# Latent preparation of an RWKV-7 mixer: norms ahead of partial products, one product to ScalarE, bonus and lower exclusive sums to GpSimd

## The chip, the core and the metric

The kernel runs on one core of a Trainium2 chip. The core's engines work side by side, each on its own queue of instructions, and wait for one another on semaphores: TensorE (PE; its weight loads are shown apart as PEld), VectorE (DVE), ScalarE (ACT), GpSimd (POOL), and SyncE (SP), which here only issues transfers. The time is the device time of one execution in microseconds (us); the median of several runs counts.

## The reference, cut to what matters

The program computes a block with a retention mixer, an RWKV-7 mixer and a mixture of experts, and behind it two layers of another model. The change touches one stage: it prepares, for the 256 latent tokens and 8 heads of 64, the operands of the RWKV-7 scan. In the reference this is:

```python
def rwkv_prepare(u, w0, w2, a0, a2, g2, k_k, k_a, r_k):
    ...
    def decay(wl, w0_d, w2_d):
        w_log = -jax.nn.softplus(-(w0_d + jnp.tanh(wl) @ w2_d)) - 0.5
        return heads(jnp.exp(-jnp.exp(w_log)))

    iclr = jax.nn.sigmoid(a0 + al @ a2)
    kk = heads(k * k_k)
    kk = kk / jnp.maximum(jnp.linalg.norm(kk, axis=-1, keepdims=True), 1e-12)
    k_mod = heads(k * (1.0 + (iclr - 1.0) * k_a))
    r, v = heads(r), heads(v)
    bonus = (jnp.sum(r * k_mod * r_k.reshape(RWKV_HEADS, RWKV_DIM), axis=-1, keepdims=True) * v).reshape(B, T, -1)
    ...
    return (r, decay(wl_f, w0[0], w2[0]), decay(wl_b, w0[1], w2[1]), k_mod, v, -kk, kk * heads(iclr), g_f, g_b, bonus)
```

The scan is done in chunks of 64 tokens, so the decays' logarithms are summed within each chunk, inclusive and exclusive, forwards for one direction and backwards for the other. Beside this, the stage makes `silu(c) @ w_mod` for the second half of the modulation.

## The kernel before

The program is a row of stages. Each opens a block in which every engine has its own list of instructions, written out by hand in the order in which it runs, and all engines meet at a barrier between stages. The stage at issue is `rwkv_prepare_stage` (from L1001), called at L1597 for the latent tokens; behind it comes `rwkv_chunks_stage` (L1294), the scan itself.

All tiles are float32 with channels on the 128 partitions. The 8 heads are worked off in 4 pairs p. Partitions 0 to 63 (`lo`) hold the forward direction of a decay, 64 to 127 (`hi`) the backward one. The steps, by engine:

- TensorE: the decays' pre-activations (L1075), those of `iclr` (L1079), the sums of squares of the keys (L1086, products with 2 columns). Then `partial(0)` and `partial(1)`, each 8 products of a weight slot (512 columns, 32 output rows, helper L183) for the modulation; the spread of the 16 norms over the partitions (L1099); `partial(2)` and `partial(3)`; `double(0)` (L1122 to L1135), which copies a pair of operands into PSUM for both directions; 16 products with one column that turn the partials (L1144); `double(1)` to `double(3)`; at the end one product to keep the engine busy (helper L162). `double(1)` waits until ScalarE has copied the result of L1144 (`second_read`).
- ScalarE: sigmoids of the decays (L1160), the squares of the keys (L1168), the sigmoids of `iclr` (L1173), after a load of another function table the square root (L1176), copies of the partials (L1180), after another table load for each pair three exponentials (L1198, L1199, L1201), which wait for `sums_ready`.
- VectorE: keys times k_k (L1250); `scan(p)`, the inclusive sums (L1215) and two small copies of the chunks' totals (L1221, L1222); `sums(p)`, the exclusive sums: one subtraction for `lo` (L1228), two for `hi` (L1230) and an addition for `hi` (L1233); the norm's clip and reciprocal (L1255, L1256, then `norm_ready`); the normed keys (L1259), `bb` (L1263), `kmod` in two steps (L1265, L1266); the bonus products (L1269), blocks 0 and 1 there, 2 and 3 behind `sums(2)`; `scale(p)` (L1243, L1244, L1246), four products of a doubled pair in PSUM with the exponentials. `scale(p)` waits for the doubling and for the exponentials of its pair; `scan(p+2)` and `sums(p+2)` come behind `scale(p)`, because there are two buffers of sums only.
- GpSimd: the product of silu (L1057), and three small operations on the modulation (L1060 to L1064).
- SyncE: three small transfers and the loads of weight slots as they come free (L121).

## Time and profile before

| | us |
|---|---|
| median of 3 runs | 1829.65 |
| lowest, highest | 1828.99, 1830.1 |
| the profiled execution | 1836.64 |
| its span | 1834.6 |
| TensorE busy | 1645.0 |
| VectorE busy | 727.8 |
| ScalarE busy | 371.8 |
| GpSimd busy | 77.2 |

The profiled execution's mean granted TensorE clock was 0.959 of full speed; a granted clock of 1.00 is 2.4 GHz, of 0.50 is 1.2 GHz. The stage runs from 374.08 us of the span, the first instruction of TensorE and of VectorE in it, to 413.74, the end of VectorE's last product. A timeline merges neighbouring instructions of the same line, xN is their number; TensorE does each float32 product as two instructions in the record. The idle time in brackets is the engine's own just before the row, with what ended it.

### The profile page before, as it was taken

To read this page: it belongs to the slowest core of one execution; us is meant where nothing else is said; L and a number is where in the kernel's file an instruction comes from. 1 tells how busy PE (TensorE), PEld (TensorE's weight loads), DVE (VectorE), ACT (ScalarE), POOL (GpSimd) and SP (SyncE) were. 2 spreads that over 40 slices of the span, in tenths; PEclk is the share of its full clock that TensorE was granted. 3 is DMA by queue.
4 is the path that set the end of the run, shared out by engine and by line. 5 is a ranking of instruction groups with operands and counts; after the bars stand their busy time and mean duration, and the time that the engine had idled before them with its cause. 6 is when DMAs were issued, how large, how long until landed. Compare 5 with 4: busy or idle time off the path is not lost.

```text
span 1834.6 us, 29021 instructions
## 1 busy us (share of the span) xinstructions
PE 1645.0 (90%) x12736; PEld 1064.6 (58%) x12736; DVE 727.8 (40%) x1326; ACT 371.8 (20%) x870; POOL 77.2 (4%) x94
## 2 busy tenths in 40 slices
PE   9999998988999876676666999999999999999998
PEld 5665557948835322121112386769984577679963
DVE  2005465675563100000000235556664255646663
ACT  2110133544422201010000224320010225210000
POOL 0000003304220000000000000000000000000000
PEclk9999998998998999888888999999999999999999
DMA  8621020040086999999999932224454532135450
GB/s 368 252 100 47 11 110 2 4 184 3 4 346 265 429 430 431 430 430 431 430 430 431 397 149 92 92 92 179 150 224 180 205 132 72 68 120 202 184 195 23
DMA packets 35583, 381.90 MB, mean 208 GB/s; under 512 B 6977, under 2 KB 10433, under 8 KB 12673
## 3 DMA queue, kind: packets, MB, share of 16 engines
q1 hardware_dynamic: 35458, 380.04, 51.2%
q8 instruction: 101, 1.65, 0.4%
q14 instruction: 24, 0.20, 0.0%
HBM read 378.98 MB, written 1.05 MB: 207 GB/s over the span
## 4 chain that ended last, share of the span: by engine, by line
PE 45%; DMA 17%; DVE 3%; ACT 2%; issue 1%; DVEq 0%; PEldq 0%
DMA arena<-in_w_moe 17%; PE psum L2959 15%; PE psum L3021 7%; PE psum L2340 6%; PE psum L2343 3%; PE psum L2009 2%; PE psum L162 2%; PE psum L2493 2%; PE psum L2481 1%; PE psum L2041 1%; PE psum L1976 1%; PE psum L2460 1%; PE psum L1956 1%; PE psum L2369 0%; PE psum L2446 0%
## 5 line engine op out<-in xcount | busy, mean ns | idle before, releaser
L2959 PE MATMUL psum<-arena 128*128 128x128 f32 x1408 | 165.2, 275 | 1.7 <-DVE arena L3157 1.7
L2959 PEld LDWEIGHTS psum<-arena 128*128 128x128 f32 x1408 | 161.0, 192 | 2.0 <-issue 2.0
L2157 DVE COPY arena<-psum 128x512 f32<-128x512 f32 x16 | 11.1, 691 | 373.2 <-PE psum L2009 373.2
L2959 PE MATMUL psum<-arena,weight_ring 128*128 128x128 f32 x1056 | 127.9, 277 | 6.3 <-DVE arena L3195 4.2
L2959 PEld LDWEIGHTS psum<-arena,weight_ring 128*128 128x128 f32 x1056 | 123.4, 194 | 8.6 <-issue 5.8
L1371 PE MATMUL psum<-arena 64*64 64x64 f32 x3328 | 109.0, 222 | 10.9 <-POOL arena L1542 8.1
L2340 PE MATMUL psum<-arena,weight_ring 128*128 128x256 f32 x512 | 118.5, 382 | 0.3 <-ACT arena L2555 0.3
L1371 PEld LDWEIGHTS psum<-arena 64*64 64x64 f32 x3328 | 101.5, 137 | 17.3 <-POOL arena L1542 8.6
L2340 PEld LDWEIGHTS psum<-arena,weight_ring 128*128 128x128 f32 x512 | 94.5, 189 | 19.1 <-issue 2.9
L2009 PE MATMUL psum<-arena 128*32 128x512 f32 x480 | 68.4, 701 | 36.8 <-DMA arena<-in_w_moe 36.8
L3140 DVE TENSOR_TENSOR arena<-weight_ring 128x1024 f32<-128x1024 f32 (+1 forms) x72 | 81.2, 1128 | 51.0 <-PE psum L3021 51.0
L2009 PE MATMUL psum<-weight_ring,arena 128*32 128x512 f32 x544 | 68.3, 632 | 27.7 <-DMA weight_ring<-in_w_moe 27.2
L3021 PE MATMUL psum<-arena 128*128 128x512 f32 x176 | 78.7, 593 | 0.4 <-DVE arena L3140 0.4
L1976 PE MATMUL psum<-arena 128*128 128x512 f32 x128 | 61.0, 620 | 18.8 <-ACT arena L2092 16.9
L2343 PE MATMUL psum<-weight_ring,arena 128*128 128x512 f32 (+1 forms) x192 | 72.3, 524 | 2.7 <-DVE arena L2796 2.7
L2080 ACT ACTIVATE arena<-psum 128x256 f32<-128x256 f32 x16 | 6.1, 384 | 288.7 <-PE psum L2021 288.7
L2009 PEld LDWEIGHTS psum<-arena 128*32 128x32 f32 x480 | 14.2, 118 | 85.1 <-DMA arena<-in_w_moe 56.0
L2009 PEld LDWEIGHTS psum<-weight_ring,arena 128*32 128x32 f32 x544 | 16.0, 113 | 77.4 <-DMA weight_ring<-in_w_moe 41.1
L467 PE MATMUL psum<-arena,weight_ring 128*128 128x256 f32 x256 | 59.0, 393 | 1.3 <-PEq L208 1.3
L3021 PE MATMUL psum<-weight_ring,arena 128*128 128x512 f32 x132 | 60.1, 592 | 0.0
L162 PE MATMUL psum<-arena 128*128 128x512 f32 x106 | 54.2, 649 | 5.4 <-DVE arena L1246 4.4
L3021 PEld LDWEIGHTS psum<-arena 128*128 128x128 f32 x176 | 33.3, 190 | 43.2 <-issue 41.1
(498 smaller groups left out, 2333.7 us busy)
## 6 DMA issues: line engine op xcount, KB each, us to landing
weight_ring<-in_w_moe SPq DMA_DIRECT2D x50, 2048.0 KB, 44.9
arena<-in_w_moe SPq DMA_DIRECT2D x46, 2048.0 KB, 44.3
weight_ring<-in_w_in SPq DMA_DIRECT2D x23, 2048.0 KB, 11.4
weight_ring<-in_w_mod SPq DMA_DIRECT2D x12, 2048.0 KB, 11.8
weight_ring<-in_w_gate SPq DMA_DIRECT2D x12, 2048.0 KB, 7.9
weight_ring<-in_w_up SPq DMA_DIRECT2D x12, 2048.0 KB, 7.9
weight_ring<-in_w_down SPq DMA_DIRECT2D x12, 2048.0 KB, 7.9
weight_ring<-in_w_out SPq DMA_DIRECT2D x6, 2048.0 KB, 7.8
```

The lines of the kernel that those rows point to most:

```text
L162: nc.tensor.matmul(K.ps[:, bank, :], K.ident, K.ident.unsqueeze(1).broadcast_to([P, 4, P]), start=True, stop=True, skip_group_check=True)
L467: last = nc.tensor.matmul(bank[:, 0:T], w[:, k, P * b:P * b + P], hT[:, k, T:2 * T], start=(k == 0), stop=(k == KT - 1), skip_group_check= ...
L1371: last = nc.tensor.matmul(K.ps[half[d], bank, to:to + HD], lhs(d, h), rhs(d, h), start=True, stop=True, skip_group_check=True)
L1956: last = nc.tensor.matmul(spot(q, d), K.h2[:, t, P * d:P * d + P], sel[:, t, cols], start=(t == 0), stop=(t == 1), skip_group_check=True)
L1976: last = nc.tensor.matmul(K.ps[:, 2 * t + n, :], scatter_to[:, e // 4 % 2, e % 4, P * t:P * t + P], parts[:, n, :], start=(e == 0), stop=( ...
L2009: last = nc.tensor.matmul(K.ps[strip(j), 4, :], xsT[:, e // 4 % 2, k, strip(e % 4)], w[:, i, j, :], start=(k == 0), stop=(k == KT - 1), sk ...
L2340: last = nc.tensor.matmul(K.ps[:, bank, 0:T], w[:, k, P * b:P * b + P], hT[:, k, :], start=(k == 0), stop=(k == KT - 1))
L2343: last = nc.tensor.matmul(K.ps[:, bank, 0:width], hT[:, k, P * b:P * b + P], w[:, k, 0:width], start=(k == 0), stop=(k == KT - 1))
L2493: last = nc.tensor.matmul(K.ps[:, out_bank(t, n), :], K.mixT[:, k, P * t:P * t + P], ws[n][:, k, :], start=(g == 0 and k == 0), stop=(g == ...
L2959: last = nc.tensor.matmul(K.ps[:, bank, P * n:P * n + P], lhs, rhs, start=(n == 0 and k == 0 and name in ("m1", "m5", "m6")), stop=(k == 3 ...
L3021: return nc.tensor.matmul(K.ps[:, int(name[1]) - 1, :], lhs, rhs, start=(j == 0), stop=(j == NFT // 2 - 1), skip_group_check=True)
L3140: nc.vector.tensor_tensor(out, x, y, op).then_inc(sums_ready, 1)
```

## The change

- TensorE: in place of `partial(0)` and `partial(1)` one product to keep it busy (helper L162) stands ahead of the spread of the norms; all four partials stand behind the spread.
- ScalarE: four Identity activations write a new tile `rate` = iclr * k_a + (1 - k_a), between `iclr` and the square root; behind the square root four Copy activations write r * r_k into `K.prod`; the copy of `partial(0)` moves behind the exponentials of pair 0.
- VectorE: `kmod` is one product, rate * k. The bonus products are gone. `sums(p)` has no subtraction for `lo`, and waits before its last addition for GpSimd (`below_ready`).
- GpSimd: 1 - k_a (128x4) first; after silu, `below(p)`, the subtraction for `lo` (64x512), once `scan(p)` is done; ahead of `below(2)` and of `below(3)` one half each of the bonus, `K.prod` times `kmod` (128x512).

```diff
@@ GpSimd
+                def below(p):
+                    pool.wait_ge(scanned, p + 1)
+                    if p >= 2:
+                        pool.wait_ge(scaled, p - 1)
+                    nc.gpsimd.tensor_tensor(exc[lo, p % 2], inc[lo, p % 2], pair(sg, p)[lo], ALU.subtract).then_inc(below_ready, 1)
+
+                nc.gpsimd.tensor_tensor(rest, K.ones[:, 0:4], K.vecs[:, 2, :], ALU.subtract).then_inc(rest_ready, 1)
                 pool.wait_ge(sig_ready, 1)
                 nc.gpsimd.tensor_tensor(K.silu, K.silu, sig, ALU.mult).then_inc(silu_ready, 1)
+                for p in range(2):
+                    below(p)
+                pool.wait_ge(r_scaled, 4)
+                pool.wait_ge(ready["k"], 1)
+                for p in range(2, 4):
+                    nc.gpsimd.tensor_tensor(K.prod[:, 2 * p - 4:2 * p - 2, :], K.prod[:, 2 * p - 4:2 * p - 2, :],
+                                            kmod[:, 2 * p - 4:2 * p - 2, :], ALU.mult)
+                    below(p)
@@ TensorE
-                if lat:
-                    pe.wait_ge(silu_ready, 1)
-                    for c in range(2):
-                        pe.wait_ge(sg_ready, 2 * c + 2)
-                        partial(c)
+                keep_busy(nc, K, 3, 1)
                 pe.wait_ge(norm_ready, 1)
...
                 if lat:
+                    pe.wait_ge(silu_ready, 1)
                     pe.wait_ge(sg_ready, H)
-                    for c in range(2, 4):
+                    for c in range(4):
                         partial(c)
@@ ScalarE
+                act.wait_ge(rest_ready, 1)
+                act.wait_ge(iclr_ready, 4)
+                for b in range(4):
+                    nc.scalar.activation(rate[:, b, :], iclr[:, b, :], ACT.Identity, bias=rest[:, b:b + 1],
+                                         scale=K.vecs[:, 2, b:b + 1]).then_inc(rate_ready, 1)
                 act.wait_ge(ss_made, 1)
...
-                if lat:
-                    keep_part(0)
+                for b in range(4):
+                    nc.scalar.activation(K.prod[:, b, :], K.rT[:, b, :], ACT.Copy, scale=K.vecs[:, 3, b:b + 1]).then_inc(r_scaled, 1)
                 for p in range(4):
                     if lat and p == 1:
+                        keep_part(0)
                         keep_part(1)
@@ VectorE
-                    link(nc.vector.tensor_tensor(e[lo], i[lo], g[lo], ALU.subtract))
...
+                    dve.wait_ge(below_ready, p + 1)
                     nc.vector.tensor_tensor(i[hi], e[hi], g[hi], ALU.add).then_inc(sums_ready, 1)
...
-                dve.wait_ge(ready["b"], 1)
-                link(nc.vector.scalar_tensor_tensor(iclr, iclr, -1.0, spread(2), ALU.add, ALU.mult))
-                nc.vector.scalar_tensor_tensor(kmod, iclr, 1.0, k, ALU.add, ALU.mult).then_inc(ready["k"], 1)
...
-                bonus(0)
-                bonus(1)
+                dve.wait_ge(rate_ready, 4)
+                nc.vector.tensor_tensor(kmod, rate, k, ALU.mult).then_inc(ready["k"], 1)
                 for p in range(4):
                     scale(p)
                     if p < 2:
                         scan(p + 2)
                         sums(p + 2)
-                    if p == 0:
-                        bonus(2)
-                        bonus(3)
```

TensorE's instructions from the sums of squares to the first doubling, before (`arena` is on-chip memory, `weight_ring` the weight slots):

```order
L1086 MATMUL psum<-arena 128x2 x8
L183 MATMUL psum<-weight_ring,arena 32x512 x16
L1099 MATMUL psum<-arena 64x128 x16
L183 MATMUL psum<-weight_ring,arena 32x512 x16
L1122 MATMUL psum<-arena 128x256 x2
```

And the same place after; L1106, L1115 and L1139 are the former L1086, L1099 and L1122:

```order
L1106 MATMUL psum<-arena 128x2 x8
L162 MATMUL psum<-arena 128x512
L1115 MATMUL psum<-arena 64x128 x16
L183 MATMUL psum<-weight_ring,arena 32x512 x32
L1139 MATMUL psum<-arena 128x256 x2
```

Sixteen of the partials' products moved from ahead of the norms' spread to behind it, and one product of 512 columns stands in their place.

GpSimd's instructions in the stage after (L1067 is 1 - k_a, L1069 silu, L1065 `below`, L1075 the bonus); before there were only those that are now L1069 and L1080 to L1084:

```order
L1067 TENSOR_TENSOR arena<-arena 128x4
L1069 TENSOR_TENSOR arena<-arena 128x8 [waits stage1_dve_step]
L1065 TENSOR_TENSOR arena<-arena 64x512 [waits stage5_s1_scanned] x2
L1075 TENSOR_TENSOR arena<-arena 128x512 [waits stage1_squares_summed,stage5_s1_r_scaled]
L1065 TENSOR_TENSOR arena<-arena 64x512 [waits stage1_hT_made,stage5_s1_scanned]
L1075 TENSOR_TENSOR arena<-arena 128x512
L1065 TENSOR_TENSOR arena<-arena 64x512 [waits stage1_hT_made,stage5_s1_scanned]
L1080 TENSOR_TENSOR arena<-arena 128x16 [waits stage5_s1_second_read,stage1_latent_scaled_by_act]
```

The second L1075 has no wait of its own: it follows `below(2)` at once. (Semaphores are named after the first stage that used them.)

## Rows read from the trace of the kernel before

**Rows 1.** Chain of waits, 480 to 600 us: start, length (us), what; its first piece.

```profile
581.01 0.04 issue
```

**Rows 2.** The page: what the DMA engines moved, in 40 slices of 45.9 us.

```profile
GB/s 368 252 100 47 11 110 2 4 184 3 4 346 265 429 430 431 430 430 431 430 430 431 397 149 92 92 92 179 150 224 180 205 132 72 68 120 202 184 195 23
```

**Rows 3.** Timeline of TensorE: start, us, engine line op out<-in xcount [idle before <-releaser].

```profile
379.60 2.12 PE L1086 MATMUL psum<-arena 128*128 128x2 f32 x16
...
381.65 5.10 PE L183 MATMUL psum<-weight_ring,arena 128*32 128x512 f32 x32
...
386.68 1.97 PE L1099 MATMUL psum<-arena 128*64 128x128 f32 x32
...
388.58 3.64 PE L183 MATMUL psum<-weight_ring,arena 128*32 128x512 f32 x32
...
392.15 0.70 PE L1122 MATMUL psum<-arena 64*128 64x256 f32 x4
...
394.34 3.73 PE L1144 MATMUL psum<-arena 128*128 128x1 f32 x32
...
398.40 1.22 PE L1122 MATMUL psum<-arena 64*128 64x256 f32 x4 [0.32 <-issue]
...
411.40 1.56 PE L162 MATMUL psum<-arena 128*128 128x512 f32 x2 [4.44 <-DVE arena L1246]
```

**Rows 4.** Timeline of ScalarE, 379 to 384 us.

```profile
379.91 1.62 ACT L1173 ACTIVATE arena<-psum,arena 128x256 f32<-128x256 f32 x4
...
381.55 1.28 ACT L1176 ACT_TABLE_LOAD   x1
...
382.84 0.18 ACT L1176 ACTIVATE arena<-psum 128x16 f32<-128x16 f32 x1
```

**Rows 5.** Timeline of VectorE, 383 to 414 us.

```profile
383.14 0.17 DVE L1255 TENSOR_SCALAR arena<-arena 128x16 f32<-128x16 f32 x1 [0.62 <-ACT arena L1176]
...
394.55 0.69 DVE L1243 TENSOR_TENSOR arena<-psum,arena 128x512 f32<-128x512 f32 x1
...
397.14 1.23 DVE L1215 TENSOR_TENSOR_SCAN arena<-arena 128x512 f32<-128x512 f32 x1
...
399.52 0.88 DVE L1230 TENSOR_TENSOR arena<-arena 64x256 f32<-64x256 f32 x2
...
401.16 0.88 DVE L1269 SCALAR_TENSOR_TENSOR arena<-arena 128x256 f32<-128x256 f32 x2
...
402.27 0.69 DVE L1243 TENSOR_TENSOR arena<-psum,arena 128x512 f32<-128x512 f32 x1 [0.23 <-PE psum L1135]
...
408.87 0.69 DVE L1243 TENSOR_TENSOR arena<-psum,arena 128x512 f32<-128x512 f32 x1
...
412.47 1.27 DVE L1246 TENSOR_TENSOR arena<-psum,arena 128x512 f32<-128x512 f32 x2
```

**Rows 6.** Stretches: us, busy PE, PEld, DVE, ACT, POOL, then granted clock, DMA share, GB/s.

```profile
381.30:384.70 3.40, 3.40 (x19) 1.11 (x22) 2.61 (x8) 1.70 (x3) 0.00 (x0) 0.51 0.99 424
...
384.70:388.10 3.40, 3.40 (x46) 1.78 (x40) 1.04 (x2) 2.96 (x4) 0.00 (x0) 1.00 1.02 347
...
398.30:401.70 3.40, 3.30 (x20) 2.06 (x24) 3.16 (x9) 0.54 (x2) 0.95 (x3) 0.50 0.04 14
...
411.90:415.30 3.40, 1.70 (x8) 0.67 (x8) 1.84 (x4) 0.00 (x0) 0.00 (x0) 0.51 0.00 0
```

**Rows 7.** GpSimd's groups by line and shape: count, busy us, mean ns, idle before.

```profile
L1542 POOL TENSOR_TENSOR arena<-arena 128x512 f32<-128x512 f32 x40 | 43.6, 1091 | 33.4 <-PE psum L1371 33.1 <-ACT arena L1493 0.4
...
L1057 POOL TENSOR_TENSOR arena<-arena 128x8 f32<-128x8 f32 x1 | 1.1, 1082 | 22.5 <-ACT arena L1166 22.5
...
L1060 POOL TENSOR_TENSOR arena<-arena 128x16 f32<-128x16 f32 x1 | 0.2, 216 | 20.4 <-ACT arena L1191 20.4
```

**Rows 8.** Timelines of VectorE and of GpSimd, 525 to 537 us.

```profile
525.59 0.88 DVE L1872 SCALAR_TENSOR_TENSOR arena<-arena 128x256 f32<-128x256 f32 x2
...
531.92 2.35 POOL L1798 TENSOR_TENSOR arena<-arena 128x1024 f32<-128x1024 f32 x1 [16.88 <-ACT arena L1832]
...
532.36 4.71 DVE L1872 SCALAR_TENSOR_TENSOR arena<-arena 128x256 f32<-128x256 f32 x2
```

More of the change, by code:

```diff
@@ L1022, in rwkv_prepare_stage @@
     norm = A.temp(2, H)
+    rate, rest = A.temp(4, T), A.temp(4)
     tok = slice(T * s, T * s + T)
```

14 lines of the change are left out of this document (7 added, 7 removed).

## The prediction

> **What bounds the kernel now.** I read the waits first, then the timelines of the four engines between 374 and 414 us (the latent preparation), then the granted clock of the same stretch, and last the chain of waits. The chain as recorded starts only at 581.01 us [rows 1], so it says nothing about this stage; what the stage is worth has to be read from its own timelines. All engines leave it together through a barrier, no weight transfer is under way from 400 to 500 us (3 and 4 GB/s in the two slices behind it [rows 2]), and so I take every microsecond by which the last VectorE product (end 412.47 + 1.27 = 413.74 us [rows 5]) moves as one that the whole kernel moves.
>
> Within the stage two paths alternate. Up to 394.5 us they are balanced: TensorE does two partial products (381.65), the spread of the norms (386.68), two more partials (388.58) and the first doubling (392.15, over at 394.34) [rows 3]; VectorE ends its keys and bonus work at the same moment and starts scale(0) at 394.55 [rows 5]. Note what the first pair of partials does there: it fills the time in which TensorE would wait for the norms. From 394.55 on VectorE is the bound: it is busy to 413.74 but for one wait of 0.23 us on the second doubling [rows 5].
>
> **The change, part by part.** All of it is summed as the new start of scale(0), then the way from there to the end.
>
> *Root later on ScalarE.* Four Identity activations of 128x256 (the rate) go between the last iclr and the square root's table load. The four sigmoids of that size take 1.62 us, the load 1.28, the root 0.18 [rows 4]. Root done: 383.02 + 1.6 = 384.65; norm_ready after the clip and reciprocal: 383.60 + 1.6 = 385.2 [rows 4, 5]. Before, this hid under partials that ran until 386.7; now they are gone and it is bare.
>
> *Spread of the norms earlier.* It can start at 385.25 instead of 386.68. At the full clock it takes 1.97 us less a little overlap [rows 3], ending 387.2. The clock decides what is left of this. It falls at 381.3, after the 2-column products of L1086 [rows 3, 6]. Before, TensorE then worked without a gap and the clock was back at 384.7 [rows 6]. Now it has one warming product (1.56 us where the clock fell during it, more at half [rows 3]) and then nothing until 385.25. In the stretch of 411.9 to 415.3 it was likewise busy for only 1.70 of 3.40 us, and there the clock stayed at 0.50 until 418.7 [rows 6]. I take that: low until 388.1. Then 2.85 us give 1.42 us of work, the other 0.55 run at full clock, end 388.65, which is just where it ended before. So the 1.4 us that the reordering gives are taken back.
>
> *Four partials behind the norms instead of two.* Two take 3.64 us at full clock (388.58 to 392.15 plus the tail [rows 3]); four take 7.2 to 7.3. First doubling starts at 395.95 and ends 2.2 us later, at 398.15 (392.15 to 394.34 before [rows 3]). scale(0) starts at 398.2 instead of 394.55: **+3.65**. With the clock back at 384.7 it would be 387.2 + 7.3 + 2.2 = 396.7: **+2.2**. Weights for the partials are no new wait: the first four-slot read had none at 381.65, and all are read later than before.
>
> *Keys' rate by ScalarE, bonus by GpSimd.* VectorE loses one 128x1024 operation and the four bonus products (one pair 0.88 [rows 5]), about 3 us in all. The first two bonuses and the 128x1024 lie ahead of scale(0), where VectorE now waits for TensorE from about 392.5 to 398.2: worth nothing. The second pair lies after sums(2) and is 1.1 us with the wait behind it (401.16 to 402.27 [rows 5]): that is on the path.
>
> *Lower exclusive sums by GpSimd.* VectorE loses a 64x512 subtraction (0.7) per pair and gets a wait for GpSimd in its place; the next scale and ScalarE's exponentials queue behind that wait. GpSimd has done no such subtraction here. Nearest row: 128x512, 1.09 us [rows 7]. If both engines ran freely, GpSimd (0.05 + 1.09) would be done before VectorE's two copies and two upper subtractions (0.40 + 0.88), and a pair gains 0.7. But GpSimd's 128x8 product at 377.01 took 1.08 us where its 128x16 addition takes 0.22 [rows 7], as long as a scan of VectorE's runs (1.22, rows of the same form in [rows 5]), and VectorE's L1872, 0.88 for two, took 4.71 for two beside GpSimd's 128x1024 products [rows 8]. Operations of VectorE with two SBUF inputs and those of GpSimd take turns. Then a pair costs 0.05 + 1.09 + 0.88 + 0.7 = 2.8, against 2.76 before (398.37 to 401.13): nothing gained. In the trace no engine works on one half of the partitions while the other works on the other half, so both ends stay: 0 to -0.7 for each of pairs 2 and 3; I take 0, since the rows on turns are of these very kinds. (Pairs 0 and 1 end before anything waits for them.) The Trainium skill, page "SBUF — State Buffer", section "SBUF: two separate sides", says that the pair of ports which VectorE and GpSimd share is an exclusive lock held for the whole instruction, and that a VectorE operation with two SBUF inputs needs it. By that rule the partition halves don't matter and the end at 0 holds; without it the total below would be 0.7 less. The trace's 4.71 us agree.
>
> *The second bonus product in the way.* GpSimd issues prod(2:4), a 128x512 product, straight behind below(2). VectorE's two upper subtractions and the addition want the same turns: one of them gets 1.09 us later. So sums(2) costs 2.8 + 1.09 = 3.9 instead of 2.76 plus the bonus' 1.14: from scale(0) to scale(1) VectorE needs 3.82 (394.55 to the scan's end 398.37) + 3.9 = 7.75, before 7.72. Bounds -1.1 (no turn lost) to +0.
>
> *TensorE on the same stretch.* Between first and second doubling stand the 1-column products (394.34 to 398.07) and ScalarE's copy (to 398.4), 4.05 us, then the doubling, 3.65 us at the half clock (398.40 to 402.05) or 2.2 at the full one [rows 3]. The clock fell at 398.3 behind those thin products [rows 6] and will again. 7.7 us: it gates scale(1) at the same moment as VectorE. So even if GpSimd took no turn, scale(1) would start no earlier: **+0.05** at best estimate.
>
> *scale(1) to the end.* 6.60 us to scale(2) and 4.87 us to the end before [rows 5]; the same with turns taken, 5.9 and 4.87 without. **0** (or -0.7). ScalarE's four Copy activations for the bonus (1.6 us) lie at 384.7 to 386.3, and its exponentials for pair 0 are done by 389.5: hidden by 8 us. GpSimd's additions to the second modulation come after below(3) instead of at 398.4; they are used behind the next stage. Transfers on SP: the third and fourth w_mod loads are released up to 5 us later, into the 100 idle us.
>
> **Sum:** 3.65 + 0.05 + 0 = +3.7 us. The profiled execution has a span of 1834.6 us and a time of 1836.64; it would be 1840.3. On the median of the runs, 1829.65, it gives 1833.3. About 0.2% (3.66 us) is what a measurement of this kernel can tell from no change, so the forecast stands on that bound.
>
> **Rivals.**
> 1. *The clock is back at 384.7.* For: the stretch begins with full-array work. Against: row 411.90 [rows 6]. scale(0) +2.2; then VectorE bounds: +2.25, time 1831.9. Where GpSimd also takes no turns, +0.1 to +1.5: about 1830.4. Chance 0.22.
> 2. *Low until 388.1, but no turns.* +3.65 - 0.7 = +2.95: 1832.6. Chance 0.12.
> 3. *Slower: the clock stays low through the partials too.* Place: TensorE, 388.1 to 391.5. TensorE's work from 385.25 on would not bring it back. Price: 3.4 us at half, 1.7 lost, total +5.4: 1835.0. It decides if the granted clock is 0.5 after 388.1. For: the stretch starts with a gap, as none did here before the clock rose at 384.7. Against: the stretch of 381.3 was followed by the full clock with such 32-column products alone [rows 3, 6]. The Trainium skill, page "TensorE: Matmul & The Clock Gate", section "What's actually happening", has the throttled state as the default, released by activity. It gives no other time than this rival or the forecast. Chance 0.13.
> 4. *Faster, or the change doesn't bite on the path.* It needs GpSimd without turns, the clock back at 384.7 and thin products that don't lower it: 387.2 + 7.3 + 2.2, then 6.25, 5.9 and 4.87 us, end at 413.8, so +0.1; and beyond that the next stage, which now starts in the low stretch of 411.9 to 418.7, starting at the full clock, worth up to 3 us. Chance of faster by over 0.2%: 0.05.
>
> **How the numbers follow.** Forecast (low to 388.1, turns taken) 0.48, half of it on either side of +3.66. Same: 0.24 + 0.22 + 0.12 = 0.58; slower: 0.24 + 0.13 = 0.37; faster 0.05. The range goes from +0.2 (rival 1 at its cheap end) to +5.5 (rival 3): 1829.8 to 1835.2.
>
> **What would show it.** In the profile after: root at 384.65 and a gap of TensorE from 383.5 to 385.2; granted clock 0.5 from 381.3 to 388.1; scale(0) at 398.2 with VectorE idle 5 to 6 us ahead of it, released by TensorE; the upper subtractions after scan(2) stretched to 3 us in all; last scale ending near 417.4. The prediction is wrong if scale(0) starts before 396.5, if the upper subtractions take 0.88 us beside GpSimd's, or if the shift of 3.7 us at the stage's end isn't found at the kernel's end.

## The result, and the profile after

The changed kernel is slower: its time is 1.0034 of the time before, 95% interval 1.0022 to 1.0046, 12 runs of each on the same chip. That is +6.2 us (4.0 to 8.4). The medians were 1838.24 and 1832.12 us. Single runs of one kernel spread far more than the three that were shown ahead of the prediction: 1828.6 to 1838.2 before, 1832.0 to 1841.5 after. Its page begins:

```profile
span 1837.8 us, 29037 instructions
...
PE 1649.6 (90%) x12738; PEld 1071.2 (58%) x12738; DVE 726.0 (40%) x1317; ACT 375.4 (20%) x878; POOL 84.4 (5%) x101
```

The span is only 3.2 us longer than in the profiled execution before, but that one happened to be slow for its kernel (1836.64 us against a median of 1832.12). The stage itself tells more. It lasts from 374.18 to 420.73, 46.55 us; before it lasted 39.66. So +6.9 us arose in it. On the way to the kernel's end 3.7 us of that were given back in this pair, 2.9 of them between 520 and 534 us: the execution before waited 2.14 us there for a weight slot and then had its clock down for 3.4 us, the one after waited 0.88 us and had its clock up. Such differences come and go between executions: in the three other profiles of the changed kernel the same wait was 2.74, 2.35 and 2.07 us. The 12 runs average over them, and their +6.2 us come close to the stage's mean loss of 6.0 us (four profiles after, two before; below).

TensorE in the stage after, the answer to [rows 3] (start, us, engine line op, idle before and its releaser). L1106, L1115, L183, L1139 and L1161 are the 2-column products, the norms' spread, the partials, the doublings and the 1-column products:

```profile
379.71 2.09 PE L1106 MATMUL psum<-arena 128*128 128x2 f32 x16
...
381.66 2.06 PE L162 MATMUL psum<-arena 128*128 128x512 f32 x2
...
385.92 3.68 PE L1115 MATMUL psum<-arena 128*64 128x128 f32 x32 [2.20 <-DVE arena L1280]
...
389.53 8.08 PE L183 MATMUL psum<-weight_ring,arena 128*32 128x512 f32 x64
...
397.54 0.70 PE L1139 MATMUL psum<-arena 64*128 64x256 f32 x4
...
399.62 4.99 PE L1161 MATMUL psum<-arena 128*128 128x1 f32 x32
...
404.94 1.23 PE L1139 MATMUL psum<-arena 64*128 64x256 f32 x4 [0.32 <-issue]
```

The partials that used to fill 381.65 to 386.7 are one warming product of 2.06 us; then TensorE waits 2.20 us. The spread takes 3.68 us, not 1.97. The four partials end at 397.5, and the doubling that they hold up ends at 399.8. The 1-column products take 4.99 us where they took 3.73.

ScalarE, the answer to [rows 4]: the rate's four activations (L1195) take 2.08 us, and push the square root from 382.84 to 385.10.

```profile
380.00 1.61 ACT L1190 ACTIVATE arena<-psum,arena 128x256 f32<-128x256 f32 x4
...
381.71 2.08 ACT L1195 ACTIVATE arena<-arena 128x256 f32<-128x256 f32 x4
...
383.81 1.28 ACT L1198 ACT_TABLE_LOAD   x1
...
385.10 0.18 ACT L1198 ACTIVATE arena<-psum 128x16 f32<-128x16 f32 x1
```

VectorE, the answer to [rows 5]. L1267 is the first product of a scale, L1238 a scan, L1246 its second small copy, L1253 and L1257 the upper half of the sums, L1270 the last products of a scale:

```profile
385.40 0.17 DVE L1279 TENSOR_SCALAR arena<-arena 128x16 f32<-128x16 f32 x1 [1.56 <-ACT arena L1198]
...
399.83 0.69 DVE L1267 TENSOR_TENSOR arena<-psum,arena 128x512 f32<-128x512 f32 x1 [6.57 <-PE psum L1152]
...
402.42 1.22 DVE L1238 TENSOR_TENSOR_SCAN arena<-arena 128x512 f32<-128x512 f32 x1
...
403.88 1.14 DVE L1246 COPY arena<-arena 64x8 f32<-64x8 f32 x1
...
405.05 1.72 DVE L1253 TENSOR_TENSOR arena<-arena 64x256 f32<-64x256 f32 x2
...
406.80 0.69 DVE L1257 TENSOR_TENSOR arena<-arena 64x512 f32<-64x512 f32 x1
...
409.01 0.69 DVE L1267 TENSOR_TENSOR arena<-psum,arena 128x512 f32<-128x512 f32 x1 [1.52 <-PE psum L1152]
...
415.87 0.69 DVE L1267 TENSOR_TENSOR arena<-psum,arena 128x512 f32<-128x512 f32 x1
...
419.46 1.27 DVE L1270 TENSOR_TENSOR arena<-psum,arena 128x512 f32<-128x512 f32 x2
```

scale(0) starts at 399.83, after a recorded idle time of 6.57 us that TensorE's doubling ends; before it started at 394.55 without one. scale(1) waits 1.52 us for the second doubling, where it waited 0.23. The small copy L1246 took 0.17 us before and takes 1.14 now, the upper subtractions of pair 2 1.72 instead of 0.88.

GpSimd, the answer to [rows 7]. L1065 is the lower subtraction, L1075 half of the bonus:

```profile
382.55 1.26 POOL L1065 TENSOR_TENSOR arena<-arena 64x512 f32<-64x512 f32 x1 [3.01 <-DVE arena L1238]
...
403.72 1.25 POOL L1065 TENSOR_TENSOR arena<-arena 64x512 f32<-64x512 f32 x1 [9.22 <-DVE arena L1238]
...
404.94 1.08 POOL L1075 TENSOR_TENSOR arena<-arena 128x512 f32<-128x512 f32 x1
```

And the stretches around the clock's fall, the answer to [rows 6] (us, busy TensorE, its weight loads, VectorE, ScalarE, GpSimd, granted clock, DMA share, GB/s). The clock is at 0.50 for three stretches on end, 381.4 to 391.6, and once more from 401.9 to 408.7:

```profile
381.40:384.80 3.40, 2.31 (x5) 0.73 (x4) 2.37 (x3) 3.29 (x6) 1.26 (x1) 0.50 0.99 424
...
384.80:388.20 3.40, 2.29 (x22) 2.29 (x24) 1.97 (x5) 3.36 (x8) 0.00 (x0) 0.50 0.64 275
...
388.20:391.60 3.40, 3.40 (x26) 1.59 (x26) 1.92 (x2) 1.76 (x3) 0.00 (x0) 0.50 0.02 5
...
391.60:395.00 3.40, 3.40 (x36) 0.96 (x32) 1.66 (x2) 1.32 (x3) 1.09 (x1) 1.00 0.00 0
...
401.90:405.20 3.30, 2.98 (x16) 2.92 (x17) 3.09 (x5) 0.18 (x1) 1.48 (x2) 0.50 1.00 427
```

### The profile page after: what moved, and what is told of

It reads as the page before. It is cut to its first block, busy times and chain, and to the rows that moved or that the text cites. A ratio compares the mean times of both kernels' runs of the same rounds, so it can differ in the third digit from the quotient of the medians.

```text
span 1837.8 us, 29037 instructions
## 1 busy us (share of the span) xinstructions
PE 1649.6 (90%) x12738; PEld 1071.2 (58%) x12738; DVE 726.0 (40%) x1317; ACT 375.4 (20%) x878; POOL 84.4 (5%) x101
## 4 chain that ended last, share of the span: by engine, by line
PE 47%; DMA 15%; DVE 3%; ACT 2%; issue 1%; DVEq 0%; PEldq 0%
PE psum L2971 15%; DMA arena<-in_w_moe 10%; PE psum L3033 7%; PE psum L2352 6%; DMA weight_ring<-in_w_moe 5%; PE psum L2355 3%; PE psum L2021 3%; PE psum L2053 2%; PE psum L2505 2%; PE psum L1988 2%; PE psum L162 2%; PE psum L2493 1%; PE psum L1968 1%; PE psum L2472 1%; PE psum L2381 0%
## 5 line engine op out<-in xcount | busy, mean ns | idle before, releaser
L2971 PEld LDWEIGHTS psum<-arena 128*128 128x128 f32 x1408 | 161.1, 192 | 2.0 <-issue 2.0
L1383 PEld LDWEIGHTS psum<-arena 64*64 64x64 f32 x3328 | 101.5, 137 | 17.4 <-POOL arena L1554 8.6
L1988 PE MATMUL psum<-arena 128*128 128x512 f32 x128 | 63.1, 638 | 18.8 <-ACT arena L2104 16.8
L1988 PEld LDWEIGHTS psum<-arena 128*128 128x128 f32 x128 | 24.6, 202 | 62.1 <-ACT arena L2104 35.6
L162 PE MATMUL psum<-arena 128*128 128x512 f32 x108 | 55.3, 649 | 5.9 <-DVE arena L1270 4.7
```

What stands on the lines that cost most here:

```text
L162: nc.tensor.matmul(K.ps[:, bank, :], K.ident, K.ident.unsqueeze(1).broadcast_to([P, 4, P]), start=True, stop=True, skip_group_check=True)
L1383: last = nc.tensor.matmul(K.ps[half[d], bank, to:to + HD], lhs(d, h), rhs(d, h), start=True, stop=True, skip_group_check=True)
L1988: last = nc.tensor.matmul(K.ps[:, 2 * t + n, :], scatter_to[:, e // 4 % 2, e % 4, P * t:P * t + P], parts[:, n, :], start=(e == 0), stop=( ...
L2971: last = nc.tensor.matmul(K.ps[:, bank, P * n:P * n + P], lhs, rhs, start=(n == 0 and k == 0 and name in ("m1", "m5", "m6")), stop=(k == 3 ...
```

## The experiments

Three things changed at once: TensorE's order, ScalarE's load ahead of the root, and GpSimd's share of VectorE's work. The experiments undo or do one at a time. For each kernel I read from its profile when the norms' reciprocal started, when scale(0) and scale(1) began and when the stage ended, all from the stage's first instruction, and for how long the clock was low between the 2-column products and the first doubling (the moment at which it goes down is called the fall here). Where a kernel was profiled more than once, each profile has its row.

| kernel | reciprocal | clock low | scale(0) | to scale(1) | stage | time against before (95%) |
|---|---|---|---|---|---|---|
| before | 9.27 | 3.4 | 20.47 | 7.72 | 39.66 | |
| before again | 9.25 | 3.4 | 20.47 | 7.62 | 39.57 | |
| after | 11.43 | 10.2 | 25.65 | 9.18 | 46.55 | 1.0034 (1.0022 to 1.0046) |
| after, 2nd | 11.43 | 10.2 | 25.62 | 9.18 | 46.53 | |
| after, 3rd | 11.43 | 6.8 | 25.32 | 7.69 | 44.73 | |
| after, 4th | 11.43 | 6.8 | 25.07 | 7.69 | 44.48 | |
| order back | 11.42 | 0 | 19.49 | 7.97 | 39.18 | 1.0004 (0.9987 to 1.0021) |
| order only | 9.25 | 3.4 | 22.30 | 7.75 | 41.53 | 1.0015 (1.0000 to 1.0030) |
| order only, 2nd | 9.26 | 6.8 | 22.83 | 7.56 | 41.87 | |
| order and rate | 11.43 | 10.2 | 25.40 | 9.18 | 46.05 | 1.0023 (1.0009 to 1.0037) |
| rate behind root | 9.90 | 3.4 | 22.80 | 7.78 | 42.31 | 1.0015 (1.0000 to 1.0030) |
| two warmers | 11.44 | 3.4 | 24.57 | 9.17 | 45.47 | 1.0027 (1.0013 to 1.0042) |
| two warmers, 2nd to 4th | 11.4 | 0; 3.4; 6.8 | 22.94; 24.55; 24.64 | 7.79; 7.70; 7.69 | 42.44; 43.97; 44.04 | |
| rate only | 11.42 | 3.4 | 20.36 | 7.70 | 39.53 | |
| lower sums only | 9.91 | 6.8 | 22.15 | 7.65 | 41.53 | |
| bonus only | 9.25 | 6.8 | 22.14 | 7.03 | 40.65 | |
| bonus first | 11.44 | 10.2 | 25.45 | 9.17 | 46.34 | |
| thin products later | 9.26 | 0 | 18.73 | 6.60 | 36.81 | 0.9988 (0.9976 to 1.0001) |

Two things have to be held apart in this table. The clock's fall lies elsewhere from one execution to the next, and by itself moves scale(0): with the old order and a clock low for 0, 3.4 or 6.8 us it comes 18.73 (thin products later), 20.47 (before) or 22.15 us in (lower sums only), 1.7 us for each 3.4. And the times are averages over such executions. So I trust the timed ratios for the size, and the profiles for which step is late.

Two profiles compare well only if the fall lies at the same place, counted from the stage's first instruction. Three groups do:

- Fall 7.0 to 7.2 us in: before 20.47 us to scale(0) and a stage of 39.66, rate only 20.36 and 39.53, after 25.65 and 46.55.
- Fall 6.7 us in: lower sums only (the old order) 22.15 and 41.53, order only in its second profile 22.83 and 41.87, order and rate 25.40 and 46.05. With the fall at 6.8, bonus first has 25.45 and 46.34.
- Fall 9.4 us in: order only in its first profile 22.30 and 41.53, after in its fourth 25.07 and 44.48.

So the late root adds 2.6 us to scale(0) under the new order and nothing under the old one, and GpSimd's work adds 0.3 us to the stage (bonus first against order and rate).

### The order back

```diff
-                keep_busy(nc, K, 3, 1)
+                pe.wait_ge(silu_ready, 1)
+                for c in range(2):
+                    pe.wait_ge(sg_ready, 2 * c + 2)
+                    partial(c)
...
-                    for c in range(4):
+                    for c in range(2, 4):
```

> The changed kernel with TensorE's order of before: partials 0 and 1 ahead of the norms' spread, 2 and 3 behind it, no warming product; ScalarE's and GpSimd's new work stays. The stage (first instruction to the end of the last scale product) lasts 39.66 us before and 46.55 after. Theory (TensorE's order and the clock that it loses are the cause): scale(0) starts within 0.6 us of before (20.5 us into the stage), the clock is back after one low stretch, the stage lasts about 40.2 us, and the time is within 0.1% of the kernel before (1829 to 1834 us beside it). Rival (ScalarE's late root and GpSimd's turns cost most of it): the stage stays above 43 us and the time stays 3 us or more above before.

Measured: ratio 1.0004 (+0.7 us, -2.4 to +3.8): the loss is gone at best estimate, although ScalarE and GpSimd still have all their new work. scale(0) came at 19.49 us, a microsecond earlier than expected. This profile had no fall ahead of the first doubling, which flatters its stage (rate only, with the same order and root and 3.4 us of low clock, had 20.36); the ratio is not flattered. TensorE in it (partials, spread, partials):

```profile
379.50 3.64 PE L183 MATMUL psum<-weight_ring,arena 128*32 128x512 f32 x32
...
383.83 1.97 PE L1119 MATMUL psum<-arena 128*64 128x128 f32 x32 [0.69 <-DVE arena L1283]
...
385.73 3.64 PE L183 MATMUL psum<-weight_ring,arena 128*32 128x512 f32 x32
```

Of the 2.2 us of idle time ahead of the spread 0.69 are left, in an execution whose partials ran at full clock (3.64 us): the two early partials cover the later root. The theory stands. Its rival (late root and turns cost most of it alone) wanted a stage above 43 us and has 39.18; the time alone would not refute it, since its 3 us lie inside the interval.

### The order alone, twice

```diff
-                    for c in range(2):
-                        pe.wait_ge(sg_ready, 2 * c + 2)
-                        partial(c)
+                keep_busy(nc, K, 3, 1)
...
-                    for c in range(2, 4):
+                    for c in range(4):
```

> The kernel before with TensorE's new order alone (one warming product, the norms' spread, then four partials; the copy of partial 0 behind the exponentials of pair 0). Root and norms come as early as before (9.5 us into the stage). Theory (order and clock): TensorE's idle time in the stretch after the first clock fall is shorter than in the changed kernel (norms ready 2.2 us earlier), so scale(0) comes at 22 to 24.5 us (before 20.5, after 25.65), and the stage lasts 42 to 44 us: time +2.5 to +4 us against before. Rival (the order is harmless with an early root): stage within 1 us of 39.66.

> TensorE's new order alone, a second profile (the first: fall at 9.5 us into the stage, 3.4 us low, scale(0) at 22.3). With the fall at 7 us: theory (the gap counts, and it is only about 0.1 us long here, since the norms are ready at 9.3 us and the warming product ends at 9.5) one low stretch, scale(0) at 22.3 to 22.8; rival, three stretches and scale(0) at 23.5 or later.

Measured: 1.0015, +2.7 us (0 to 5.5), scale(0) 22.30 and 22.83 us in, stages 41.53 and 41.87. The first was a little below the range of 42 to 44 that I had given. The second profile had its fall at 6.7 us and the clock low for 6.8 us, where I had expected 3.4, and TensorE had no idle time at all ahead of the spread: a gap is not needed for the clock to stay down longer. scale(0) came 0.03 us outside that expectation. At best estimate the order alone is under half of the loss; its interval reaches nearly all of it.

### Order and rate together, and the rate moved

> The kernel before with two things of the change: TensorE's new order, and the keys' rate by four Identity activations ahead of the square root (GpSimd only makes 1 - k_a). Bonus and lower sums stay with VectorE. Theory (the late root under the new order costs the larger part, GpSimd's turns next to nothing): norms ready 11.4 us into the stage, scale(0) at 24 to 25.7 us, time 4.5 to 6 us above before (ratio 1.0025 to 1.0034). Rival (it takes GpSimd's work as well): time 2 to 3 us above before, ratio 1.0015, as with the order alone.

Without any of GpSimd's new work but 1 - k_a, the stage is 46.05 us, scale(0) at 25.40, the spread at half clock throughout (3.68 us): the changed kernel's picture. The ratio, 1.0023, is a little under the range I expected, and its interval reaches both the changed kernel's and that of the order alone. Of the timed numbers alone, this doesn't separate the two; the profiles do, since this one and the second of the order alone have their fall at the same place, 6.7 us in. TensorE's spread with the order alone, second profile, without idle time ahead of it:

```profile
382.90 3.68 PE L1095 MATMUL psum<-arena 128*64 128x128 f32 x32
```

And with order and rate (spread, 1-column products):

```profile
384.84 3.68 PE L1098 MATMUL psum<-arena 128*64 128x128 f32 x32 [1.76 <-DVE arena L1260]
...
398.29 5.23 PE L1144 MATMUL psum<-arena 128*128 128x1 f32 x32
```

The late root opens the gap of 1.76 us, the clock is low for 10.2 us instead of 6.8, and the 1-column products, shifted back, meet the next fall: 2.6 us up to scale(0), 1.6 more up to scale(1), 4.2 in the stage.

The reverse, in the changed kernel:

```diff
-                act.wait_ge(rest_ready, 1)
-                act.wait_ge(iclr_ready, 4)
-                for b in range(4):
-                    nc.scalar.activation(rate[:, b, :], ...)
                 act.wait_ge(ss_made, 1)
                 nc.scalar.activation(norm, ..., ACT.Sqrt).then_inc(root_ready, 1)
+                act.wait_ge(rest_ready, 1)
+                act.wait_ge(iclr_ready, 4)
+                for b in range(4):
+                    nc.scalar.activation(rate[:, b, :], ...)
```

> The changed kernel with one thing undone: the four Identity activations (keys' rate) stand behind the square root instead of ahead of it, so the norms are ready 9.3 us into the stage instead of 11.4. TensorE's new order and all of GpSimd's work stay. Theory (new order and late root multiply: together they leave TensorE idle for over 2 us, and the clock then stays low into the partials): TensorE's idle time ahead of the norms' spread is about 0, scale(0) comes at about 22.3 us as in the kernel with the order alone, and the time is 2.5 to 4 us above before instead of 6. Rival (GpSimd's turns cost the rest): the time stays 5 us or more above before.

Ratio 1.0015, +2.7 us (0 to 5.5): the same as the order alone, and at best estimate about half of the loss is gone with one move on ScalarE, though GpSimd keeps all its work. The rival of the expectation (GpSimd's turns cost the rest, 5 us or more) is at the edge of the interval; against it speak the stage of 42.31 us and scale(0) at 22.80, and the 0.3 us of GpSimd's work above. TensorE (warming product, spread, partials):

```profile
379.62 1.10 PE L162 MATMUL psum<-arena 128*128 128x512 f32 x2
...
382.50 3.37 PE L1115 MATMUL psum<-arena 128*64 128x128 f32 x32 [1.77 <-DVE arena L1280]
...
385.79 7.07 PE L183 MATMUL psum<-weight_ring,arena 128*32 128x512 f32 x64
```

I had expected no idle time ahead of the spread; it was 1.77 us, because the clock had not fallen yet and the warming product took 1.10 us, not 2.06. scale(0) is where I expected it, within 0.5 us. The norms came 0.65 us later than with the order alone: VectorE's small copy was caught behind GpSimd's lower subtraction (1.14 us), just ahead of the clip.

> The kernel before with only the keys' rate by ScalarE ahead of the square root (and 1 - k_a by GpSimd). Root 2.1 us later under the old order of TensorE. Theory (the two early partials cover the later root): the spread of the norms starts at 12.6 to 14.3 us into the stage as in the kernel before, straight behind the partials with no idle time of TensorE, and scale(0) at 19.5 to 22.2. Rival (a late root costs 2 us by itself): idle time ahead of the spread, scale(0) 2 us later.

The rate alone under the old order: spread at 12.60 us as before, scale(0) at 20.36, stage 39.53. The late root by itself costs nothing (one profile, not timed, with its fall where before has it). So order and late root each have a price only through the other: the order uncovers the root, the rate's activations then make it late.

### What the clock has to do with the gap

```diff
-                keep_busy(nc, K, 3, 1)
+                keep_busy(nc, K, 3, 2)
```

> The changed kernel with two warming products of 512 columns instead of one ahead of the norms' spread, so that TensorE has 4.1 us of work at the half clock in place of 2.06. Nothing else moves. Theory (the gap of TensorE keeps the clock low): there is one low stretch instead of three in a row, the spread takes about 2.0 instead of 3.68 us and the four partials 7.3 instead of 8.1, the stage is 2 to 3 us shorter than the 46.55 of the changed kernel in an execution with the same clock fall, and the time is 3 to 4 us above before. Rival (the clock was low for another reason): stage and time as in the changed kernel.

> Two warming products, a second profile. If the clock falls 7 to 7.3 us into the stage, behind the 2-column products: theory (the gap keeps it low) one low stretch of 3.4 us, spread about 2 us long, scale(0) at 23.2 to 23.8 us; rival (the work doesn't bring it back) low for 6.8 us or more, spread 3.7 us, scale(0) at 25 us or later.

> Two warming products, a third profile; expectations as in the second: with the fall at 7 to 7.3 us into the stage, one low stretch and scale(0) by 23.8 us by the theory, three stretches and 25 us or later by the rival.

> Two warming products, a fourth profile; expectations as in the second: with the fall at 7 to 7.3 us into the stage, one low stretch and scale(0) by 23.8 us by the theory, three stretches and 25 us or later by the rival.

> The changed kernel once more, for a second profile: how much of its stage hangs on where the clock falls. Theory (order, late root and clock): scale(0) 24 to 25.7 us into the stage and the stage 45 to 46.6 us, with the clock low for 6.8 us or more around the norms' spread; if the clock does not fall there, scale(0) at about 23.7. Rival (the first profile was an outlier): scale(0) below 23 us.

> The changed kernel, a third profile. If the gap keeps the clock low: at least 6.8 us low around the norms' spread wherever the fall lies in the first 10 us of the stage, stage 44 us or more. If the difference to two warming products was chance of the moment of the fall: some profile with 3.4 us low or none and a stage of 42 to 43.5 us.

> The changed kernel, a fourth profile; expectations as in the third.

> The kernel before once more, for a second profile. Theory: its stage also hangs on where the clock falls, but less: scale(0) 19.5 to 22.2 us into the stage (19.49, 20.47, 22.14 and 22.15 have been seen in kernels with its order), stage 38.5 to 41.5 us. Rival: it is steady at 39.66.

With one warming product and the late root, six profiles (four of the changed kernel, order and rate, bonus first) have the clock low for 10.2, 10.2, 6.8, 6.8, 10.2 and 10.2 us, and never less. With two warming products it was 3.4, 0, 3.4 and 6.8 us. None of these four had its fall at 7 us into the stage, for which the expectation was made, so the test as I had planned it never took place. The changed kernel's further profiles came within what I had expected of them: never less than 6.8 us low, and stages of 46.53, 44.73 and 44.48 us. The granted clock in the third profile of the changed kernel (stretches as above): low from 380.0 to 386.8, the spread within it.

```profile
376.60:380.00 3.40, 1.87 (x11) 1.04 (x10) 2.99 (x4) 3.29 (x8) 1.26 (x1) 0.99 1.04 443
...
380.00:386.60 6.60, 4.83 (x40) 3.68 (x44) 3.07 (x6) 5.78 (x10) 0.00 (x0) 0.50 0.42 179
...
386.70:390.00 3.30, 3.30 (x36) 0.90 (x32) 2.38 (x3) 0.81 (x2) 0.74 (x1) 0.99 0.00 0
```

And TensorE in the second profile with two warming products (warming products, spread, partials), with no fall at all and a gap of 2.45 us none the less:

```profile
379.61 1.96 PE L162 MATMUL psum<-arena 128*128 128x512 f32 x4
...
384.02 1.97 PE L1115 MATMUL psum<-arena 128*64 128x128 f32 x32 [2.45 <-DVE arena L1280]
...
385.92 7.07 PE L183 MATMUL psum<-weight_ring,arena 128*32 128x512 f32 x64
```

The stages average 44.0 us with two products (four profiles) against 45.6 (four of the changed kernel), but none of the four has its fall where a profile of the changed kernel has it: 12.8, none, 12.0 and 8.5 us in against 7.2, 7.1, 9.9 and 9.4. So these averages do not separate the second product from the place of the fall. The timed ratio, 1.0027 (+4.9 us), can't be told from 1.0034. The expected 2 to 3 us did not come. What stays open is why the clock stays down for 3.4, 6.8 or 10.2 us; that the gap prolongs it is likely by these profiles and not shown. One more thing goes with it, without any gap: in before, before again and rate only the fall came 7.0 to 7.2 us in, with 0.5 to 0.9 us of the 2-column products still to run, and the clock was low for 3.4 us; in lower sums only, bonus only and the second profile of the order alone it came 6.6 to 6.7 us in, with 1.4 to 1.6 us of them still to run, and it was low for 6.8. Not open is what it costs: at the half clock the spread takes 3.68 instead of 1.97 us, and the 1-column products with the doubling behind them 9.2 instead of 7.7 us from scale to scale.

Both profiles of the kernel before have scale(0) at 20.47 us and stages of 39.66 and 39.57. That is no sign of a steady kernel: both had their fall at nearly the same place, 7.2 and 7.0 us in.

### GpSimd's share

> The kernel before with only the lower exclusive sums given to GpSimd. Theory (VectorE and GpSimd take turns, and the second small copy of VectorE is caught by it): each pair's sums last as long as or 0.1 to 0.3 us longer than before: scan's end to the addition's end 2.76 before, 2.9 here; stage 39.7 to 40.4 us. Rival (they run side by side): 2.05 us a pair, stage 38.9 to 39.0 us.

The kernel before with only the lower subtraction on GpSimd. VectorE from the second small copy of pair 2 on:

```profile
396.45 1.14 DVE L1234 COPY arena<-arena 64x8 f32<-64x8 f32 x1
...
397.62 0.88 DVE L1241 TENSOR_TENSOR arena<-arena 64x256 f32<-64x256 f32 x2
...
398.54 0.69 DVE L1245 TENSOR_TENSOR arena<-arena 64x512 f32<-64x512 f32 x1
```

From the scan's end (396.22) to the end of the addition (399.23) it takes 3.01 us, before 2.76. The engines take turns: the subtraction of GpSimd (1.26 us) holds up VectorE's second copy (1.14 us instead of 0.17), and only then come the upper subtractions at their usual 0.88. Nothing is gained by moving the operation; 0.25 us are lost. The stage, 41.53 us, was above the expected range; the clock was low for 6.8 us ahead of the first doubling in this execution, and from scale(0) on it took 19.4 us against 19.2.

> The kernel before with only the bonus given to ScalarE (r times r_k, behind the root) and GpSimd (times the keys, both halves as soon as the keys are there). VectorE has 1.8 us less to do behind the keys. Theory (TensorE gates both scale(0) and scale(1) at that moment already in the kernel before): the stage stays within 0.3 us of 39.66, and the 0.9 us of the second bonus pair turn into a longer wait for the second doubling, 1.1 us instead of 0.23. Rival (VectorE's work is the bound): the stage is 0.9 to 1.1 us shorter.

The first product of scale(0) and of scale(1) with only the bonus moved:

```profile
394.50 0.69 DVE L1251 TENSOR_TENSOR arena<-psum,arena 128x512 f32<-128x512 f32 x1 [0.85 <-PE psum L1141]
...
401.53 0.69 DVE L1251 TENSOR_TENSOR arena<-psum,arena 128x512 f32<-128x512 f32 x1 [0.46 <-PE psum L1141]
```

7.03 us between them instead of 7.72, with 0.46 us of wait left. So my theory was wrong by half: 0.7 us were gained, since the second doubling took 2.98 us and not 3.65; the clock fell about 1 us after it had begun, and not ahead of it. The stage's 40.65 us again hold a longer fall; from scale(0) to the end it took 18.5 us, 0.7 less than before. One profile, not timed.

```diff
                 for p in range(2, 4):
                     nc.gpsimd.tensor_tensor(K.prod[:, 2 * p - 4:2 * p - 2, :], ...)
+                for p in range(2, 4):
                     below(p)
```

> The changed kernel with both halves of the bonus product on GpSimd ahead of the third lower subtraction, so that none stands in the way of VectorE's upper ones. Theory (turns between the two engines; the second doubling gates scale(1) anyway): the two upper subtractions of pair 2 take 0.88 instead of 1.72 us, the wait for the second doubling grows by the same 0.84, and the stage stays where it was, 46.5 us, or what the clock makes of it: scale(0) to scale(1) unchanged at 9.2 if the clock falls at the same place. Rival: the stage is 0.8 us shorter for it.

As expected: the upper subtractions of pair 2 took 0.88 us again, and the wait for the second doubling grew by the same 0.83, from 1.52 to 2.35 us. From scale to scale 9.17 us, before the edit 9.18. The turn lost to the second bonus product was real, and cost nothing in this execution.

```profile
404.81 0.88 DVE L1254 TENSOR_TENSOR arena<-arena 64x256 f32<-64x256 f32 x2
...
408.76 0.69 DVE L1268 TENSOR_TENSOR arena<-psum,arena 128x512 f32<-128x512 f32 x1 [2.35 <-PE psum L1153]
```

It does not follow that it never costs anything. In the third profile of the changed kernel the second doubling ends at 402.13 us, and VectorE comes to scale(1) only at 403.04, without idle time:

```profile
401.03 1.10 PE L1152 MATMUL psum<-arena 64*64 64x256 f32 x8
...
403.04 0.69 DVE L1267 TENSOR_TENSOR arena<-psum,arena 128x512 f32<-128x512 f32 x1
```

There VectorE is the bound, its upper subtractions take 1.72 us too, and the lost turn costs about 0.8 us by my estimate (1.72 less 0.88). The fourth profile has the same picture. No run shows bonus first in such an execution.

### The 1-column products later

The order of before, the rate behind the root, the bonus on ScalarE and GpSimd, the lower sums on VectorE; and the sixteen 1-column products behind the second doubling, in a bank that scale(0) has read:

```diff
-                    pe.wait_ge(part_kept, 4)
-                    for c in range(4): ... matmul(K.ps[:, 4, ...], part[c], ...)
-                for p in range(1, 4):
+                double(1)
+                pe.wait_ge(scaled, 1)
+                for c in range(4): ... matmul(K.ps[:, 0, ...], part[c], ...)
+                for p in range(2, 4):
                     double(p)
```

> A version built on what the runs showed: TensorE's order of before up to the first doubling; the rate's four activations behind the square root; the bonus on ScalarE and GpSimd, both halves as soon as the keys are there; lower sums on VectorE. New: the sixteen 1-column products stand behind the second doubling (in the bank that scale(0) has freed) instead of between the first two. Theory (in the kernel before these products and the clock that falls behind them gate scale(1) by 0.2 us and, once the second bonus is off VectorE, by 0.5 to 1.1): scale(0) to scale(1) 6.6 us instead of 7.72 and 7.03 (bonus alone), from scale(0) to the end 18.1 us instead of 19.2; time 1 us below before, which is inside what can be measured. Rival (something else is late next, the keys or the exponentials): 7.5 us or more.

From scale(0) to scale(1) 6.60 us, from scale(0) to the end 18.08, both as expected. TensorE's second doubling and its 1-column products:

```profile
391.49 0.70 PE L1131 MATMUL psum<-arena 64*128 64x256 f32 x4 [0.77 <-issue]
...
393.58 3.73 PE L1153 MATMUL psum<-arena 128*128 128x1 f32 x32
```

VectorE's first product of scale(0) and of scale(1); the second has no idle time ahead of it:

```profile
390.86 0.69 DVE L1259 TENSOR_TENSOR arena<-psum,arena 128x512 f32<-128x512 f32 x1 [2.13 <-PE psum L1144]
...
397.46 0.69 DVE L1259 TENSOR_TENSOR arena<-psum,arena 128x512 f32<-128x512 f32 x1
```

The ratio is 0.9988 with an interval of 0.9976 to 1.0001: faster by 2.2 us at best estimate, and not clear of no change. Its stage of 36.81 us is also helped by an execution without a fall ahead of the first doubling.

## Why the prediction was wrong

The sign of the sum was right (+3.7 us), and so were most places; the size was not. The measured +6.2 us lie outside the range, which ended at +5.5. (The interval, 4.0 to 8.4, leaves out the forecast of +3.7 and not the range's end.) I had also put 0.58 on a change too small to see and 0.37 on slower. Step by step, with the profiles of after; their stages were 6.0 us longer on average than the two of before, where the sum had 3.7:

- *Root later on ScalarE.* Right in kind. I took 1.6 us for the four Identity activations, from the four sigmoids. They took 2.08. That they read on-chip memory and not PSUM does not explain it: the four Copy activations read on-chip memory as well and took 1.69. Identity has a scale and a bias per partition, the sigmoid and the Copy one of the two; whether that is the difference no run tests. The spread started 11.74 us into the stage, not 11.17: mis-sized by 0.6 us, with no cover.
- *Spread of the norms.* This is the step that failed: "low until 388.1". I let the clock come back 14.0 us into the stage, before the spread was through. In the four profiles of the changed kernel it came back 17.4, 17.4, 16.8 and 16.2 us in. The spread ran at half speed from end to end, 3.68 us each time, and the first 0.9 to 2.1 us of the partials with it. That is the mechanism of my third rival, which had the clock low for 3.4 us more; it was 3.4, 3.4, 2.7 and 2.2. Together 0.6 us of a later start, 0.2 of spread and 0.1 to 0.7 of partials made scale(0) later by 4.6 to 5.2 us against before, where the sum had 3.65: on average 1.3 us of the 2.3 that the sum lacks.
- *TensorE between the first doublings.* I took 7.7 us from scale to scale, with the 1-column products at the length that they have at full clock. In two profiles of four it was 7.69. In the other two the clock fell while they ran; they took 4.99 and 5.03 us instead of 3.73, and the doubling was slow as well: 9.18 us. I had priced the fall for the doubling alone; that is 0.7 us of the 2.3 on average. The trace of before has no such product at the half clock to price it from, and the bound was missing. The two profiles with 7.69 match my number partly by luck: there VectorE is the bound, with TensorE done 0.8 to 0.9 us earlier, and my two paths happened to be equally long. (In the sum for VectorE, 3.82 + 3.9 is 7.72 and not 7.75; nothing hangs on it.)
- *Lower exclusive sums.* The turns were right, and the forecast of no gain too. I had 0, it was +0.25 us for pair 3 (6.86 instead of 6.60 us from scale(1) to scale(2)), mostly because GpSimd's 64x512 takes 1.26 us and not 1.09.
- *The second bonus product in the way.* Right in kind: the two upper subtractions took 1.72 us (not the 3 us that I had named as a sign), and from the scan's end to the addition's it took 3.85 us, forecast 3.9. Where TensorE gated scale(1) it cost nothing, as the run with the bonus first shows; in the two other profiles it cost about 0.8 us by estimate, which the bonus off VectorE paid for.
- *Keys' rate and bonus off VectorE.* Right for the part ahead of scale(0): nothing gained, VectorE stood idle for 6.57 us there.
- *The rest of the kernel.* I let the shift pass to the end unchanged. On average it does: the stage's excess was 4.8 to 6.9 us, the time's 6.2, and from the stage's end to the first products of a weight slot behind 500 us (L183) it took 94.8 to 95.2 us in every profile of the two kernels. In a single pair of executions half can vanish behind that.

Of the rivals, the slower one came nearest (1835.0 us, +5.4), and I had given it 0.13. I had also read the three runs shown, 1829 to 1830 us, as the kernel's spread; 12 runs range over 10 us. In my fourth rival 396.7 + 6.25 + 5.9 + 4.87 is 413.7, so no change, where I wrote +0.1. And the interplay was there to see in my own steps: the root's delay and the missing partials both widen the same gap of TensorE, and where the clock falls around it moves the rest. I priced both with the fall at one place and one length of the low time.

## What to carry to other kernels

Work that an engine does while it would wait for another is cover: before it is moved, ask what it covers, and whether the same change makes the covered thing later. Here the order cost 2.7 us (0 to 5.5), the later root nothing, both together 4.2 (1.6 to 6.8), and the whole change 6.2 (4.0 to 8.4). The intervals overlap; the profiles with the fall at the same place tell them apart (stages of 41.87 and 46.05 us). So profiles of a kernel whose clock moves should be compared at the same place of the fall, or by many timed runs. A step whose clock isn't known should be priced at both levels for every operation in it, short ones with it, and moving a two-input operation from VectorE to GpSimd beside other such operations of VectorE freed no time here (3.01 us instead of 2.76).

## What the runs showed of the hardware

- A 64x8 copy of VectorE, within on-chip memory, is held up by a GpSimd operation too: 0.17 us alone, 1.13 to 1.16 us beside GpSimd's 64x512 subtraction, in every kernel that has one. In the changed kernel's pair 2 the first copy starts at 403.68, GpSimd's operation at 403.72, the second copy at 403.88: the first got through. I had counted only the operations with two inputs. The Trainium skill, page "SBUF — State Buffer", section "SBUF: two separate sides", names VectorE's operations in a two-port mode as well as those with two inputs as users of the shared pair of ports, and has float32 copies within SBUF run in that mode. The trace agrees, with these 1.14 us.
- GpSimd's subtraction over 64 partitions and 512 elements took 1.25 to 1.28 us, its product over 128 partitions and 512 elements 1.09. Every such subtraction started 0.04 or 0.05 us after VectorE's first small copy (0.17 us), so up to 0.13 us of it may be a wait; no run has it alone. Half the partitions was not less time either way.
- ScalarE's Identity with a scale and a bias per partition, 128x256 from on-chip memory: 2.08 us for four; the Copy with a scale per partition 1.69; the sigmoid with a bias per partition, from PSUM, 1.61.
- The 1-column products, one 128x128 weight load each, took 3.73 us for sixteen at the full clock and up to 5.23 with the clock down for most of them.
- The same kernel's clock falls at different places of the same stage in different executions: in the four profiles of the changed kernel it fell 7.1 to 9.9 us in, and in kernels with the old order the low time ahead of the first doubling was 0, 3.4 or 6.8 us, and scale(0) came 18.73 to 22.15 us into the stage.
